# A two-block transformer kernel on one core: x in two transfers, setup moved into the first feed-forward, and another order at each feed-forward entry

## The chip, the core and the metric

The kernel runs on one core of a Trainium2 chip. A core has five engines with instruction streams of their own: TensorE (PE, matrix products and transposes), VectorE (DVE), ScalarE (ACT), GpSimd (POOL) and SyncE (SP), which here only issues transfers. Engines wait for each other by semaphores. Transfers come from HBM through 16 DMA engines, from one queue for those that SyncE issues and one for those of ScalarE. The metric is the device time of one execution in microseconds (us), less is better.

## What is computed

The input x has 256 tokens of 1024 values in fp32. Two layers of a first block and two layers of a second block follow each other. Each layer is a gated feed-forward (hidden width 2816), a mixer and another feed-forward, so there are eight feed-forwards.

```python
def first_block(x, ...):
    cos, sin = rope_tables(positions)
    for layer in range(DEPTH):
        x = x + 0.5 * swiglu(rmsnorm(x, norm_g[layer, 0]), ffn_w_gate[layer, 0], ffn_w_up[layer, 0], ffn_w_down[layer, 0])
        x = x + hybrid_mixer(rmsnorm(x, norm_g[layer, 1]), cos, sin, w_in[layer], ...)
        x = x + 0.5 * swiglu(rmsnorm(x, norm_g[layer, 2]), ffn_w_gate[layer, 1], ffn_w_up[layer, 1], ffn_w_down[layer, 1])
...
def second_block(x, ...):
    for i in range(DEPTH):
        f = swiglu_ffn(rmsnorm_2(x, ffn1_norm_pre[i]), ffn1_w_in[i], ffn1_w_out[i])
        x = x + 0.5 * rmsnorm_2(f, ffn1_norm_post[i])
        ...
        x = x + rmsnorm_2(y, mix_norm_post[i])
        f = swiglu_ffn(rmsnorm_2(x, ffn2_norm_pre[i]), ffn2_w_in[i], ffn2_w_out[i])
        x = x + 0.5 * rmsnorm_2(f, ffn2_norm_post[i])
```

The second block has a post norm: the output of a feed-forward or mixer is normed before it is added to x.

## The kernel before

**Split products.** Every fp32 operand is split into a high part (rounded to fp32r) and a low part (the rest), and each product is three: high by high, low by high, high by low (`three`, L505 to L507). Weights stream through a ring of four slots in parts of 128 x 1024 values (512 KB). For each part SyncE issues the transfers (`load_parts`, L344) once the slot's earlier low part is made; ScalarE makes the high part `wh` (`high`, L533) when the part has landed and TensorE has started on the part three before it (the semaphore `used`); VectorE, or GpSimd from the mixers to part 3 of the next feed-forward, makes the low part `wl` (`low`, L541). The helpers take a count: `high(e, t, 2)` makes the next two parts. The Python order of the calls is the order of the instructions on each engine; there is no scheduler.

**The entry of a feed-forward.** x lies with tokens on partitions, as two halves of 128 tokens (q = 0, 1). TensorE transposes 8 blocks of each half (`pe_xt`, L638). ScalarE makes their high parts `xh` (`act_xh`, L1279, four or eight of 128 x 128 at once) and VectorE their low parts `xl` (`dve_xl`, L1782). It starts on four low parts when the four high parts are there. Then chunk 0 (the first 256 of 2816 hidden columns, four weight parts, 0 to 3) runs for q = 0, then for q = 1; the transposes of the half q = 1 stand among the parts of q = 0, behind part 1 in the first block and behind part 2 in the second. Meanwhile ScalarE sums the squares of x (`act_sum`, L1283) and takes the root (`act_root`, L1289, L1292), and loads the table of silu (`tables`, L1257). TensorE goes on with part 4 (chunk 1) and then transposes the hidden values of chunk 0 (`turn`, L661), for which ScalarE has to apply silu (`silu`, L1361) and VectorE has to multiply by the up half (`gated`, L1861). Behind that ScalarE and VectorE make `hh` and `hl` of the hidden values (`turned`). Ten more chunks and 22 down parts follow.

**The residual in the second block.** In the entries behind a mixer or feed-forward with a post norm, ScalarE squares the output in PSUM (`act_post`, L1283), VectorE multiplies it by the post gains (`gained`, L1805) and adds it to x (`added`, L1813). TensorE's transposes of that half of x wait for the addition. This holds for three feed-forward entries, at 1852, 2048 and 2632 us.

**The setup.** SyncE loads x in one transfer of 1 MB and then weight parts 0 to 3. ScalarE issues eleven small transfers: positions and lambda parameters (spread to all partitions, 128 and 256 KB), norm gains (24 KB), and eight others. VectorE computes the rotary angles (L2026 to L2041) and lambda; TensorE transposes the gains (L1204) and the small parameters (L1206), both behind the wait for all parameters, and then the first half of x; ScalarE takes two sines (L1708, L1709), copies gains and parameters, takes two exponentials (L1716, L1717), and only then starts on weight parts.

## Time and profile before

| | us |
|---|---|
| median of three runs | 2831.6 |
| lowest and highest | 2831.0 and 2835.13 |
| the profiled execution | 2832.48 |
| its span | 2830.7 |

| engine | busy us | share of the span |
|---|---|---|
| TensorE products (PE) | 2733.8 | 97% |
| VectorE (DVE) | 1580.8 | 56% |
| ScalarE (ACT) | 1463.0 | 52% |
| GpSimd (POOL) | 899.4 | 32% |

The DMA engines move 450 MB, 159 GB/s on the mean. The chain of work that ended last is 87% TensorE. Times in rows are from the start of the span; the profiled execution took 1.8 us more than its span.

### The profile page before, as it was taken

How to read it: one execution, taken by the hardware profiler on the slowest of the kernel's cores; microseconds unless marked ns; L12 is line 12 of the kernel's file. 1: busy time of each engine (PE TensorE's matmuls, PEld its weight loads, DVE VectorE, ACT ScalarE, POOL GpSimd, SP SyncE). 2: the span in 40 equal slices, each digit the busy share in tenths (PEclk: the TensorE clock that was granted, in tenths of full speed). 3: DMA queues.
4: the chain of work that ended last, by engine and by line, in shares of the span. 5: the costliest groups of instructions: out<-in, count | busy, mean ns of one | idle time of the engine just before them, and what ended most of it. 6: DMA issues, size and time to landing. Idle time of an engine off the chain costs nothing.

```text
span 2830.7 us, 46605 instructions
## 1 busy us (share of the span) xinstructions
PE 2733.8 (97%) x17368; PEld 2360.3 (83%) x17368; DVE 1580.8 (56%) x2439; ACT 1463.0 (52%) x2136; POOL 899.4 (32%) x469
## 2 busy tenths in 40 slices
PE   7999999999999999999989999999999899999999
PEld 6888897887878997878879899878778798998787
DVE  5543854545544844545546585655455466756554
ACT  5445565445445655445455644654454556446543
POOL 0007563001017666010028554720100285547200
PEclk9999999999999999999999999999999999999999
DMA  5555445655555446556558542456555585424664
GB/s 183 184 182 153 132 138 178 186 186 176 185 167 156 132 142 193 186 172 191 184 137 201 113 91 73 148 183 186 176 182 185 139 197 120 91 69 149 186 186 142
DMA packets 368426, 450.01 MB, mean 159 GB/s; under 512 B 32510, under 2 KB 266112, under 8 KB 368224
## 3 DMA queue, kind: packets, MB, share of 16 engines
q1 hardware_dynamic: 366896, 446.34, 53.6%
q8 instruction: 138, 2.26, 0.3%
q10 hardware_dynamic: 400, 0.43, 0.1%
q0 software_dynamic: 928, 0.45, 0.1%
q14 instruction: 64, 0.52, 0.1%
HBM read 446.06 MB, written 1.05 MB: 158 GB/s over the span
## 4 chain that ended last, share of the span: by engine, by line
PE 87%; DVE 5%; ACT 4%; POOL 2%; issue 1%; DMA 0%; ACTq 0%; DVEq 0%
PE PS L505 26%; PE PS L507 25%; PE PS L506 25%; POOL wl L541 2%; PE PS L661 1%; ACT wh L533 1%; ACT xh L1279 1%; DVE PS L2078 1%; DVE wl L541 1%; PE PS L1072 1%; PE PS L770 1%; PE PS L1007 1%; PE PS L1139 1%; PE PS L638 1%; PE PS L998 1%
## 5 line engine op out<-in xcount | busy, mean ns | idle before, releaser
L541 POOL TENSOR_TENSOR wl<-ring,wh 128x1024 fp32r<-128x1024 f32 (+1 forms) x348 | 835.9, 2421 | 1728.5 <-ACT wh L533 1727.4
L533 ACT ACTIVATE wh<-ring 128x1024 fp32r<-128x1024 f32 x848 | 890.4, 1055 | 919.2 <-PE PS L505 880.4
L541 DVE TENSOR_TENSOR wl<-ring,wh 128x1024 fp32r<-128x1024 f32 x500 | 611.8, 1225 | 630.8 <-ACT wh L533 630.7
L505 PE MATMUL PS<-wh,xh 128*128 128x512 f32 x1600 | 634.0, 396 | 33.2 <-DVE xl L1782 25.3
L507 PE MATMUL PS<-wh,xl 128*128 128x512 f32 x1600 | 623.2, 390 | 0.0
L506 PE MATMUL PS<-wl,xh 128*128 128x512 f32 x1600 | 622.1, 389 | 0.0
L505 PE MATMUL PS<-xh,wh 128*128 128x256 f32 x1888 | 554.4, 294 | 1.7 <-DVE xl L1782 1.7
L506 PE MATMUL PS<-xl,wh 128*128 128x256 f32 x1888 | 539.3, 286 | 0.0
L507 PE MATMUL PS<-xh,wl 128*128 128x256 f32 x1888 | 538.9, 285 | 0.0
L505 PEld LDWEIGHTS PS<-wh,xh 128*128 128x128 f32 x1600 | 301.2, 188 | 101.5 <-issue 34.9
L505 PEld LDWEIGHTS PS<-xh,wh 128*128 128x128 f32 x1888 | 367.0, 194 | 22.5 <-issue 16.2
L506 PEld LDWEIGHTS PS<-xl,wh 128*128 128x128 f32 x1888 | 367.6, 195 | 2.5 <-issue 2.4
L507 PEld LDWEIGHTS PS<-xh,wl 128*128 128x128 f32 x1888 | 367.2, 195 | 0.0
L507 PEld LDWEIGHTS PS<-wh,xl 128*128 128x128 f32 x1600 | 301.1, 188 | 63.0
L506 PEld LDWEIGHTS PS<-wl,xh 128*128 128x128 f32 x1600 | 301.7, 189 | 58.1
L505 PE MATMUL PS<-wh,hh 128*128 128x512 f32 x704 | 279.1, 396 | 0.0
L507 PE MATMUL PS<-wh,hl 128*128 128x512 f32 x704 | 278.1, 395 | 0.0
L506 PE MATMUL PS<-wl,hh 128*128 128x512 f32 x704 | 278.1, 395 | 0.0
L2078 DVE SCALAR_TENSOR_TENSOR PS<-W,cols,PS 128x256 f32<-128x256 f32 x464 | 187.2, 480 | 0.0
L507 PEld LDWEIGHTS PS<-wh,hl 128*128 128x128 f32 x704 | 132.1, 188 | 32.1
L506 PEld LDWEIGHTS PS<-wl,hh 128*128 128x128 f32 x704 | 132.2, 188 | 31.7
L505 PEld LDWEIGHTS PS<-wh,hh 128*128 128x128 f32 x704 | 132.2, 188 | 31.5
(296 smaller groups left out, 2604.6 us busy)
## 6 DMA issues: line engine op xcount, KB each, us to landing
ring<-in_ffn_w_in_dram SPq DMA_DIRECT2D x352, 256.0 KB, 3.0
ring<-in_mix_w_in_dram SPq DMA_DIRECT2D x256, 256.0 KB, 3.8
ring<-in_w_in_dram SPq DMA_DIRECT2D x200, 256.0 KB, 3.0
ring<-in_ffn_w_gate_dram SPq DMA_DIRECT2D x176, 256.0 KB, 2.9
ring<-in_ffn_w_up_dram SPq DMA_DIRECT2D x176, 256.0 KB, 3.1
ring<-in_ffn_w_down_dram SPq DMA_DIRECT2D x176, 256.0 KB, 2.7
ring<-in_ffn_w_out_dram SPq DMA_DIRECT2D x176, 256.0 KB, 2.7
ring<-in_w_branch_dram SPq DMA_DIRECT2D x32, 256.0 KB, 2.9
```

Source lines behind the costliest of these rows:

```text
L505: first_ = mm(o, w[0], x[0], start=start, stop=False, skip_group_check=True)
L506: mm(o, w[0], x[1], start=False, stop=False, skip_group_check=True)
L507: return first_, mm(o, w[1], x[0], start=False, stop=stop, skip_group_check=True)
L533: act_(dst, src, ACT.Copy).then_inc(hi_ready, 1)
L541: (engine or v_).tensor_tensor(dst, src, part_views(t, wh)[0], ALU.subtract).then_inc(lo[t.slot()], 1)
L638: ins = nc.tensor.transpose(xt_bank(q, k), src[:, q, k * P:(k + 1) * P], ident[:])
L661: ins = nc.tensor.transpose(bank(4 + c % 2, o, o + P), act2[:, c % 2, q, j * P:(j + 1) * P], ident[:])
L770: mm(bank(5, 0, n), rot[:], ybuf[:, c % 2, 0:n], start=True, stop=True).then_inc(tr[0].sem, tr[0].did("rot." + name))
L998: ins = mm(PS[0:4, 4, 0:S], pick[:, 3 - h:7 - h], sq[:, 4 * (n % 2) + h, :], start=(h == 0), stop=(h == 3))
L1007: ins = mm(bank(4, i * S, (i + 1) * S), ident[0:4, h:h + 1].to_broadcast([4, P]), rstd[0:4, 0, 0:S], start=True, stop=True)
L1072: ins = mm(PS[r, 3 + 2 * c, h * HD:(h + 1) * HD], src[c][r, h, :], ident[r, r], start=True, stop=True)
L2078: ins = v_.scalar_tensor_tensor(conv[:, b, :] if tap == TAPS - 1 else part, src, w, part, ALU.mult, ALU.add)
```

## The change

1. x comes in two transfers of 512 KB: SyncE loads the half q = 0 first, ScalarE issues the load of q = 1 behind its first high weight part. Each half has its semaphore.
2. The norm gains are ScalarE's first transfer and have a semaphore of their own. Positions and lambda parameters are issued in the first entry, behind high part 3.
3. TensorE transposes the gains, then x (q = 0), then the small parameters, then runs chunk 0. ScalarE loads the table with exp and ln first, copies the gains and starts on weight parts; it copies the small parameters inside the entry.
4. The angles are computed by VectorE in chunks 3 to 5 of the first feed-forward, the lambda products in chunk 6; the sines follow on ScalarE in chunk 8, the exponentials and the rest of lambda in the down projection.
5. In the first entry weight and activation parts alternate: high part 0, xh of q = 0 in two groups of four with high part 1 between them, then high parts 2 and 3.
6. In the other seven entries ScalarE makes all eight xh of q = 0 in one go and high part 3 behind them. In all eight, one high part and one low part that stood ahead of chunk 0's silu and gating now stand behind them.
7. In the three entries with a post norm VectorE's multiplication by the post gains for q = 1 moves behind xl 4 to 7.

```diff
         def _(sp):
-            sp.dma_start(x, a["x"].rearrange("a (t p) d -> p (a t) d", p=P)).then_inc(x_in, 16)
+            load_x(sp, 0)
...
+            pe.wait_ge(gains_in, 16)
+            for k in range(KB):
+                ins = nc.tensor.transpose(bank(1, k * ROWS1, (k + 1) * ROWS1), rows[0:ROWS1, k * P:(k + 1) * P],
+                                          ident[0:ROWS1, 0:ROWS1])
+            ins.then_inc(pro_pe.sem, pro_pe.did("gains"))
+            pe_xt_ffn(pe, 0, 0)
             pe.wait_ge(params_in, N_PARAM)
-            for k in range(KB):
-                nc.tensor.transpose(bank(1, k * ROWS1, (k + 1) * ROWS1), rows[0:ROWS1, k * P:(k + 1) * P],
-                                    ident[0:ROWS1, 0:ROWS1])
...
             if s == 0:
                 high(e, t, 1)
-            if post:
-                post(0)
-            high(e, t, 2)
-            act_xh(e, s, 0, range(4), gain)
-            high(e, t, 1)
-            act_xh(e, s, 0, range(4, KB), gain)
+                load_x(e, 1)
+                act_xh(e, s, 0, range(4), gain)
+                high(e, t, 1)
+                act_xh(e, s, 0, range(4, KB), gain)
+                high(e, t, 2)
+                load_late(e)
+                e.wait_ge(params_in, N_PARAM)
+                e.wait_ge(pro_pe.sem, pro_pe.at("small"))
+                act_(small[:], bank(3, 0, SMALL), ACT.Copy).then_inc(pro_act.sem, pro_act.did("small"))
+            else:
+                if post:
+                    post(0)
+                high(e, t, 2)
+                act_xh(e, s, 0, range(KB), gain)
+                high(e, t, 1)
...
             high(e, t, 1)
-            if s == 0:
-                tables(LN_EXP)
             act_root(e, tr, env.lay, f"{tag}.ss1", tag, 0, QT)
             tables(SILU_TANH)
-            high(e, t, 2)
+            high(e, t, 1)
...
-                high(e, t, 2)
+                high(e, t, 3 if c == 1 else 2)
                 turned(c - 1)
+                chunk(c)
...
             if s == 0:
-                low(e, t, 3)
+                low(e, t, 1)
             gained(0)
             added(0)
             dve_xl(e, s, 0, range(4), gain)
             if s == 0:
                 low(e, t, 1)
-            gained(1)
             if s < 3 * LAYERS + 1:
+                gained(1)
                 added(1)
             dve_xl(e, s, 0, range(4, KB), gain)
+            if s == 0:
+                low(e, t, 1)
+                e.wait_ge(x_in[1], 16)
+                e.sem_inc(x_upd, 2)
+                low(e, t, 1)
             if s > 3 * LAYERS:
+                gained(1)
                 added(1)
             dve_xl(e, s, 1, range(KB), gain)
-            low(e, t, 3)
+            low(e, t, 2)
...
-                low(e, t, 2)
+                low(e, t, 3 if c == 1 else 2)
                 turned(c - 1)
+                chunk(c)
```

The order of instructions on ScalarE at the program's start, before. W, small and cols hold the setup's values, masks the sines and cosines, wh the high parts of the weights:

```order
L1708 ACT_TABLE_LOAD
L1708 ACTIVATE masks<-W 128x256 [waits setup_vector]
L1709 ACTIVATE masks<-W 128x256
L1712 ACTIVATE cols<-PS 128x48 [waits setup_products,params_loaded]
L1714 ACTIVATE small<-PS 128x14
L1716 ACT_TABLE_LOAD
L1716 ACTIVATE W<-W 128x4 [waits setup_vector]
L1717 ACTIVATE gd<-gd 8x2
L533 ACTIVATE wh<-ring 128x1024 [waits weight_parts_used,weights_landed_0,setup_scalar]
```

The same place after the change:

```order
L1268 ACT_TABLE_LOAD
L1728 ACTIVATE cols<-PS 128x48 [waits setup_products]
L543 ACTIVATE wh<-ring 128x1024 [waits weight_parts_used,weights_landed_0,setup_scalar]
L332 DMA x<-in_x_dram 128x1024
L1290 ACTIVATE xh<-PS,cols 128x128 [waits activations_transposed] x4
L543 ACTIVATE wh<-ring 128x1024 [waits weight_parts_used,weights_landed_1]
L1290 ACTIVATE xh<-PS,cols 128x128 [waits activations_transposed] x4
L543 ACTIVATE wh<-ring 128x1024 [waits weight_parts_used,weights_landed_2]
L543 ACTIVATE wh<-ring 128x1024 [waits weight_parts_used,weights_landed_3]
L308 DMA W<-in_positions_dram 128x256
L308 DMA W<-in_lambda_params_dram 128x512
L1354 ACTIVATE small<-PS 128x14 [waits setup_products,params_loaded]
```

Five operations and a table load stand no more between the first copies and the first weight part; three transfers now stand between parts and activations.

VectorE at the last entry, the one at 2632 us, before (post multiplication L1805, addition L1813, xl L1782, low weight parts L541, gating L1861):

```order
L1782 SCALAR_TENSOR_TENSOR xl<-PS,cols,xh 128x128 [waits activation_high_parts_made] x4
L1805 TENSOR_TENSOR PS<-PS,post 128x512 [waits second_norm_scalar]
L1805 TENSOR_TENSOR PS<-PS,post 128x512
L1782 SCALAR_TENSOR_TENSOR xl<-PS,cols,xh 128x128 [waits activation_high_parts_made] x4
L1813 SCALAR_TENSOR_TENSOR x<-PS,rs,x 128x512 [waits second_norm_vector,second_norm_scalar]
L1813 SCALAR_TENSOR_TENSOR x<-PS,rs,x 128x512 [waits second_norm_vector]
L1782 SCALAR_TENSOR_TENSOR xl<-PS,cols,xh 128x128 [waits activation_high_parts_made] x8
L541 TENSOR_TENSOR wl<-ring,wh 128x1024 [waits weight_high_part_ready] x3
L1861 SCALAR_TENSOR_TENSOR act<-PS,rs,act 128x256 [waits second_ffn_scalar] x2
L541 TENSOR_TENSOR wl<-ring,wh 128x1024 [waits weight_high_part_ready] x2
```

The same place after the change:

```order
L1807 SCALAR_TENSOR_TENSOR xl<-PS,cols,xh 128x128 [waits activation_high_parts_made] x8
L1830 TENSOR_TENSOR PS<-PS,post 128x512 [waits second_norm_scalar]
L1830 TENSOR_TENSOR PS<-PS,post 128x512
L1838 SCALAR_TENSOR_TENSOR x<-PS,rs,x 128x512 [waits second_norm_vector,second_norm_scalar]
L1838 SCALAR_TENSOR_TENSOR x<-PS,rs,x 128x512 [waits second_norm_vector]
L1807 SCALAR_TENSOR_TENSOR xl<-PS,cols,xh 128x128 [waits activation_high_parts_made] x8
L551 TENSOR_TENSOR wl<-ring,wh 128x1024 [waits weight_high_part_ready] x2
L1892 SCALAR_TENSOR_TENSOR act<-PS,rs,act 128x256 [waits second_ffn_scalar] x2
L551 TENSOR_TENSOR wl<-ring,wh 128x1024 [waits weight_high_part_ready] x3
```

The second group of four xl moved ahead of the post multiplication, and one low weight part moved behind the gating.

ScalarE at the same entry, before (high weight parts L533, xh L1279, square of the output L1283):

```order
L533 ACTIVATE wh<-ring 128x1024 [waits weight_parts_used,weights_landed_0]
L1279 ACTIVATE xh<-PS,cols 128x128 [waits activations_transposed] x4
L533 ACTIVATE wh<-ring 128x1024 [waits weight_parts_used,weights_landed_1]
L1279 ACTIVATE xh<-PS,cols 128x128 [waits activations_transposed] x4
L1283 ACTIVATE act,ss<-PS 128x1024 [waits second_mix_products]
```

And after:

```order
L543 ACTIVATE wh<-ring 128x1024 [waits weight_parts_used,weights_landed_0]
L1290 ACTIVATE xh<-PS,cols 128x128 [waits activations_transposed] x8
L543 ACTIVATE wh<-ring 128x1024 [waits weight_parts_used,weights_landed_1]
L1294 ACTIVATE act,ss<-PS 128x1024 [waits second_mix_products]
```

The second group of four xh moved ahead of a high weight part.

## Rows read from the trace of the kernel before

**Rows 1.** What TensorE waited for, whole span: us in total, times, longest us.
```profile
PE PS L505 <- DVE xl L1782: 27.0, 16, 5.3
PE PS L661 <- DVE act L1861: 9.2, 8, 2.1
```

**Rows 2.** Timeline of the start: start, duration, instruction, count, [idle before <- releaser].
```profile
2.21 0.74 SPq L344 DMA_DIRECT2D ring<-in_ffn_w_up_dram  x1
...
11.42 1.01 PE L1204 MATMUL PS<-ident,W 6*128 6x6 f32 x8 [8.90 <-DMA W<-in_diff_subln_g_dram]
...
12.96 1.28 ACT L1716 ACT_TABLE_LOAD   x1
...
14.58 2.95 ACT L533 ACTIVATE wh<-ring 128x1024 fp32r<-128x1024 f32 x3
...
19.74 0.77 PE L505 MATMUL PS<-wh,xh 128*128 128x512 f32 x1 [5.29 <-DVE xl L1782]
...
39.07 0.63 PE L661 MATMUL PS<-ident,act 128*128 128x128 f32 x4 [2.13 <-DVE act L1861]
```

**Rows 3.** Transfers issued in 0 to 3 us; last line 17 to 24: KB, us to landing.
```profile
x<-in_x_dram SPq DMA_DIRECT2D x1, 1024.0 KB, 7.7
ring<-in_ffn_w_up_dram SPq DMA_DIRECT2D x1, 256.0 KB, 9.0
W<-in_positions_dram ACTq DMA_DIRECT2D x1, 128.0 KB, 5.8
...
ring<-in_ffn_w_up_dram SPq DMA_DIRECT2D x4, 256.0 KB, 3.7
```

**Rows 4.** Stretches: length, busy time (instructions) of PE, PEld, DVE, ACT, POOL; clock, DMA, GB/s.
```profile
5.00:10.00 5.00, 0.00 (x0) 0.00 (x0) 3.07 (x10) 1.28 (x1) 0.40 (x2) 1.00 0.98 345
...
40.00:60.00 20.00, 20.00 (x91) 16.53 (x90) 11.37 (x14) 10.40 (x14) 0.00 (x0) 1.00 0.69 213
```

**Rows 5.** Timeline of the last entry with a post norm, 2630 to 2652 us.
```profile
2630.81 1.14 ACT L1279 ACTIVATE xh<-PS,cols 128x128 fp32r<-128x128 f32 x4 [0.45 <-PE PS L638]
...
2632.48 0.47 PE L505 MATMUL PS<-wh,xh 128*128 128x512 f32 x1 [1.28 <-DVE xl L1782]
...
2633.05 1.06 ACT L533 ACTIVATE wh<-ring 128x1024 fp32r<-128x1024 f32 x1 [1.09 <-PE PS L505]
...
2635.01 1.04 ACT L1283 ACTIVATE act<-PS 128x1024 f32<-128x1024 f32 x1
...
2636.18 1.30 DVE L1805 TENSOR_TENSOR PS<-PS,post 128x512 f32<-128x512 f32 x2 [3.06 <-ACT act L1283]
...
2637.87 0.47 PE L505 MATMUL PS<-wh,xh 128*128 128x512 f32 x1 [2.39 <-DVE xl L1782]
...
2638.41 1.40 DVE L1813 SCALAR_TENSOR_TENSOR x<-PS,rs,x 128x512 f32<-128x512 f32 x2
...
2640.28 0.48 PE L505 MATMUL PS<-wh,xh 128*128 128x512 f32 x1
...
2644.07 1.10 ACT L533 ACTIVATE wh<-ring 128x1024 fp32r<-128x1024 f32 x1
...
2650.27 0.87 DVE L1861 SCALAR_TENSOR_TENSOR act<-PS,rs,act 128x256 f32<-128x256 f32 x2
...
2651.29 0.63 PE L661 MATMUL PS<-ident,act 128*128 128x128 f32 x4 [1.20 <-DVE act L1861]
```

**Rows 6.** The same stretch of the entry at 1852 us: timeline, then the stretch's busy times.
```profile
1858.09 0.76 PE L505 MATMUL PS<-wh,xh 128*128 128x512 f32 x1 [2.38 <-DVE xl L1782]
...
1861.88 0.48 PE L505 MATMUL PS<-wh,xh 128*128 128x512 f32 x1
...
1858.00:1860.00 2.00, 1.91 (x5) 1.55 (x6) 2.00 (x5) 0.00 (x0) 0.00 (x0) 0.50 0.78 257
```

**Rows 7.** First hidden transposes at two entries of the other kinds, timeline.
```profile
471.23 0.63 PE L661 MATMUL PS<-ident,act 128*128 128x128 f32 x4 [0.71 <-DVE act L1861]
...
1287.54 0.63 PE L661 MATMUL PS<-ident,act 128*128 128x128 f32 x4 [1.29 <-DVE act L1861]
```

More of the change, by code:

```diff
@@ L238, in program @@
         passed = {e: sem(f"wait_passed_{e}") for e in ("sync", "vector", "tensor", "gpsimd", "scalar")}
-        x_in = sem("x_loaded")
-        pos_in = sem("positions_loaded")
+        x_in = [sem(f"x_loaded_{q}") for q in range(QT)]
+        gains_in = sem("gains_loaded")
+        late_in = sem("positions_and_lambda_loaded")
         params_in = sem("params_loaded")
@@ L312, in load_params @@
             ld = loader(q, params_in)
[L313 to L314 removed]
+            loader(q, gains_in)(rows[0:3 * LAYERS, :], a["norm_g"].rearrange("l r d -> (l r) d"))
             ld(gd[0:8, 0, 0:LAYERS], a["gdn_a_log_2"].rearrange("l h -> h l"))
             ld(gd[0:8, 1, 0:LAYERS], a["gdn_dt_bias_2"].rearrange("l h -> h l"))
[L317 removed]
             for l in range(LAYERS):
@@ L1329, in act_mix_in, with act_ffn @@
             act_xh(e, s, 1, range(KB), gain)
-        def act_ffn(e, t, ff, tr, s, tag, gain, post=None, midway=lambda: None, more=1):
+        def act_ffn(e, t, ff, tr, s, tag, gain, post=None, midway=lambda: None, more=1, chunk=lambda c: None):
             if s == 0:
                 high(e, t, 1)
-            if post:
-                post(0)
-            high(e, t, 2)
-            act_xh(e, s, 0, range(4), gain)
-            high(e, t, 1)
-            act_xh(e, s, 0, range(4, KB), gain)
+                load_x(e, 1)
[13 more added lines that the diff above has]
+                high(e, t, 1)
             if post:
@@ L1733, in _ @@
                 g1 = cols1[:, :, 3 * lay:3 * lay + 3]
-                act_ffn(e, t, first["ffn"], tr, s, "f0", lambda k: g1[:, k, 0:1])
+                act_ffn(e, t, first["ffn"], tr, s, "f0", lambda k: g1[:, k, 0:1], None, decays if lay == 0 else lambda: None,
+                        1, angles if lay == 0 else lambda c: None)
                 act_mix_in(e, t, tr, s + 1, lambda k: g1[:, k, 1:2])
@@ L1836, in dve_mix_in, with dve_ffn @@
             dve_xl(e, s, 1, range(KB), gain)
-        def dve_ffn(e, t, ff, tr, s, tag, gain, update=None, midway=lambda: None):
+        def dve_ffn(e, t, ff, tr, s, tag, gain, update=None, midway=lambda: None, chunk=lambda c: None):
             gained, added = update or (lambda q: None, lambda q: None)
             if s == 0:
-                low(e, t, 3)
+                low(e, t, 1)
             gained(0)
@@ L2248, in _ @@
             dve_setup(e)
-            e.wait_ge(pro_act.sem, pro_act.at("small"))
+            e.wait_ge(pro_act.sem, pro_act.at("cols1"))
             def halves():
@@ L2264, in _ @@
                 t = Tiles(lay * (T1 // SLOTS), 4 if lay else 0)
-                dve_ffn(e, t, ff, tr, s, "f0", lambda k: g1[:, k, 0:1], update)
+                dve_ffn(e, t, ff, tr, s, "f0", lambda k: g1[:, k, 0:1], update,
+                        (lambda: dve_lambda(e)) if lay == 0 else lambda: None,
+                        (lambda c: dve_angles(e, c)) if lay == 0 else lambda c: None)
                 dve_mix_in(e, tr, s + 1, lambda k: g1[:, k, 1:2], dve_residual(e, ff[0], "f0.dn", lay))
```

81 lines of the change are left out of this document (46 added, 35 removed).

## The prediction

> **What bounds the kernel now.** I read three views in this order. First the table of busy time above: TensorE is busy 97% of the span, so the end moves only where TensorE stands still or runs at its lower clock. Then the list of what TensorE waited for: its two largest entries that this change can touch are waits for low parts of the activations (L1782, 16 times, 27.0 us) and for the gated hidden values (L1861, 8 times, 9.2 us) [rows 1]. Then the timeline at each of the eight feed-forward entries. At the program's start the first transposes wait 8.9 us for the last parameter transfer (11.42), ScalarE loads a table at 12.96, splits its first weight part only at 14.58, and the first product runs at 19.74 [rows 2]. Behind the start, each entry has one wait ahead of the first hidden transposes (L661), and the three entries whose residual update goes through a post norm have a wait of 2.4 us in the middle of chunk 0 [rows 5, 7].
>
> **Part 1, the start.** Removed from the path: the rotary angles, the lambda steps, two sine activations and one table load no longer stand ahead of ScalarE's first high part, and TensorE's gain transposes wait for one 24 KB transfer, not for all eleven. What is late next is weight part 0. Its second half was issued at 2.21 and landed 9.0 us later [rows 2, 3], at 11.2. It stood behind 1 MB of x and 384 KB of positions and lambda rows (128 and 256 KB). Now half of x and those 384 KB come later, about 0.91 MB less, and the queues moved 345 GB/s in this stretch [rows 4]: 2.6 us, so 8.6. From there the path to the first product is one high part 1.06 (as at 2633.05 [rows 5]), the new issue of the second half of x on ScalarE's queue, about 0.5 (an issue took 0.74 on SyncE [rows 2]), and from the start of the four high activation parts to the first product 1.67 (2630.81 to 2632.48 [rows 5]): 3.2 us. First product near 11.9, against 19.74: **7.8 us**. Ends: if part 0 lands as late as now, 14.4 and 5.3 us; if it lands as the refills later do, 3.7 us after issue [rows 3], 9.1 and 10.6 us. I take the middle, because the queue is full either way.
>
> Three new waits stand in that path. The gains: the positions, 128 KB and first on the same queue, landed after 5.8 us, at 6.6 [rows 3]; 1.0 for eight transposes and 0.2 for the copy give 7.9, under 8.6. The remaining small parameters, for which TensorE now waits just before its first product: they landed by 11.4 with 384 KB ahead of them, so at most 11.4 now, under 11.9. The second half of x, issued near 10.2: 3.7 to 7.7 us to landing [rows 3] gives 13.9 to 17.9. VectorE waits for it, with low part 3 and the low activation parts of the second token half queued behind, and TensorE reaches the second transposes 12 products after the first. The first product lasts 0.77 as the one at 1858.09 does (0.76), where the granted clock is 0.50, the 1.2 GHz level, and five products fill 1.91 us [rows 2, 6]; 12 at about 0.4 us end at 16.7. So it costs nothing to 1.2 us; I take nothing, since half the bytes of the 7.7 us row are asked for.
>
> The Trainium skill speaks against this split: "DMA: Bandwidth & Descriptors", Bandwidth, asks for transfers of at least 1 MiB, and its fit (2.0 us plus bytes over 436 GB/s) makes two halves 2.0 us dearer in sum than one whole. No row here prices the halves. Were that fixed part on the path, the forecast would be 2809.8; as the second half lands under chunk 0, I leave it out.
>
> **Part 2, the setup that moves into chunks 3 to 8 of the first feed-forward.** Some 13 VectorE steps, two sine activations and, in the down projection, seven more small steps. In a steady stretch of 20 us VectorE is busy 11.4 and ScalarE 10.4 under 20.0 of TensorE [rows 4], so 8.6 us lie free in less than two chunks, against 1 to 1.5 us added in one. Cost nothing; without this cover they would cost their own length, some 5 us in all. The order shows no table load for the sines where they now stand. Nobody needs the angles before the mixer, and GpSimd, which waits for the cosine, starts its own low parts only there.
>
> **Part 3, one high part and one low part behind the gate, in all eight entries.** Before, ScalarE made parts 5 and 6 and VectorE low parts 4, 5, 6 before the first gating; now part 6 goes behind it. From the start of high part 4 (2644.07) to the end of the gating (2650.27 + 0.87) 7.07 us pass [rows 5]. Without one high part (1.06) it is 6.0. TensorE arrives at the transposes at 2651.29 - 1.20 = 2650.09, which is 6.02 us after 2644.07. With 0.15 from gating to transposes about 0.1 of the wait stays. The three first-block entries like the one at 471.23 (0.71) lose their wait whole [rows 7]: 3 x 0.7 = **2.1**. The entry at 1287.54 (1.29 [rows 7]) gives **1.1**; the three later ones, of which the last with 1.20 is shown [rows 5], give **1.1 each**. In the first feed-forward the wait of 2.13 [rows 2] goes, since one table load goes too: **2.1**. Low part 6 is then made some 1 us after the gate, while TensorE wants it two parts (over 5 us) later, so nothing is late next.
>
> The Trainium skill ("ScalarE: Activation LUTs", What ACT_TABLE_LOAD costs, and the terms) gives a table load about 2.7 us; the load here took 1.28 [rows 2], so the trace differs, and it decides. By 2.7 the 6.0 us chain would be 7.4 and each entry would keep 1.4 of wait, and this part would give nothing.
>
> **Part 4, high parts of the whole first token half in one go, and the post gains behind the low parts, in the three post-norm entries.** Before, low activation parts 4 to 7 stood behind the post gain on VectorE (2636.18, 1.30), which waited for ScalarE's square (2635.01), which waited for high weight part 3 and four high activation parts. That made the 2.39 wait at 2637.87 [rows 5]. Now ScalarE makes the four high parts straight after the first four, in the 1.09 us in which it stood idle before 2633.05; so weight part 3 is not later and the square is 1.0 earlier, at 2634.0. VectorE makes the low parts by 2634.2, in its own idle time (3.06 before 2636.18). The gain goes to 2635.2, the addition, which no longer waits for four low parts, to 2636.4 instead of 2638.41, and ends at 2637.8. TensorE runs without the wait to about 2636.7 and is then stopped by this addition at the second transposes. The product behind them starts 0.47 after the addition (2638.41 + 1.40 to 2640.28), so at 2638.2: **2.0 us** per entry, not 2.4, because the new wait takes the place of part of the old one. In the entry at 1858.09 the same stretch took 3.79 us (1858.09 to 1861.88) against 2.41 (2637.87 to 2640.28), at a granted clock of 0.50 [rows 5, 6]. With a pause under 1 us in place of 2.4 I expect the clock to stay up: **1.4** more.
>
> **Sum.** Start 7.8 + 2.1 = 9.9; first block 2.1; then 1.1; 1858: 2.0 + 1.4 + 1.1 = 4.5; the last two 3.1 each. Together 23.8. The profiled execution took 2832.48, so 2808.7 there; on the median of the three runs, 2831.6, it is **2807.8**.
>
> **Rivals.** *Late weights* (15%): part 0 lands as late as now, because its slices on the 16 engines wait for the slowest engine and not for bytes. For: 1.97 MB stood ahead up to its landing, at 345 GB/s less than the 11.2 us it took. Against: x itself landed by 8.5. Then 2.5 more, 2810.3. *Clock* (15%): shorter waits move everything behind them, and the falls of the clock move too. One fall costs 1.4 [rows 6]; three more make 2812.0, three fewer 2803.6. What speaks for it is that the entry at 1858 fell and its twins did not, though the wait was the same. The Trainium skill, "TensorE: Matmul & The Clock Gate", What's actually happening, says that the place of a change depends on a phase that a kernel doesn't set; the unequal twins agree. *Gate no earlier* (6%): the activation then waits for something else, a product or a landing, and Part 3 brings nothing, 8.6 less: 2816.4. Against it the products of the second token half end one part (2.7 us) before the transposes. *Slower* (2%): with an earlier start TensorE stays at 1.2 GHz in the first feed-forward. A chunk lasts about 11.4 us there and would cost some 9 more; from three chunks on the gain is eaten: 2835. Against it, after the first dozen products it never fell in the first block. *Not as said*: if the second half of x lands after 17.9, TensorE waits at the second transposes and the start brings up to 3 less, within the range.
>
> **How the numbers follow.** Forecast 62%, its own range 2805.0 to 2810.3 by the two ends of the start. The range goes to three fewer falls and to three more with late weights added in part: 2802.5 to 2814. About 0.2%, 5.7 us, is what a measurement of this kernel tells from no change. Faster by more than that 0.95, within 0.03, slower 0.02; all but the last rival are faster.
>
> **What would show it.** First product between 9.1 and 14.4; table load before the first high part gone; no wait over 0.3 us at L661's successors; in the three post-norm entries no wait in the middle of chunk 0 but a short one, 0.5 to 1, before the second transposes; granted clock 1.00 near 1850. Wrong would be a first product after 15, or entries that keep their waits.

## The result and the profile after

| | before | after |
|---|---|---|
| undisturbed executions, us | 2831.0 to 2835.13 | 2803.77, 2805.36, 2807.67 |
| the profiled execution | 2832.48 | 2807.67 |
| its span | 2830.7 | 2805.9 |

The ratio of after to before is 0.9905, with a 95% interval of 0.9885 to 0.9924, so 22 to 33 us are gone by the interval, 24.8 between the two profiled executions. One further execution of the changed kernel was disturbed and is left out. The forecast was 2807.8 with a range of 2802.5 to 2814: the median of the three, 2805.36, and the profiled execution lie inside it. The signs of the terms were right, but the sizes of several were not, and they cancelled in part. The rest of this text is about those.

The page of the changed kernel first: busy time of each engine with its share and instructions, and the chain that ended last.

```profile
PE 2735.0 (97%) x17368; PEld 2363.6 (84%) x17368; DVE 1588.1 (57%) x2439; ACT 1459.5 (52%) x2134; POOL 899.6 (32%) x469
...
PE 90%; DVE 4%; ACT 3%; POOL 2%; issue 1%; DMA 0%; SPq 0%; DVEq 0%; ACTq 0%
```

TensorE is about as busy as before (2735.0 us, before 2733.8), and the span is 24.8 shorter. So the time came out of its pauses, and the chain now runs over TensorE for 90% of the span, not 87%. Next, what TensorE waited for in the changed kernel (us in total, times, longest). The lines L505, L638, L661 and L1782 of before are L515, L648, L671 and L1807 now.

```profile
PE PS L648 <- DVE sq L1800: 18.1, 6, 3.8
PE PS L515 <- DVE xl L1807: 15.7, 12, 1.6
...
PE PS L1219 <- DMA W<-in_diff_subln_g_dram: 1.9, 1, 1.9
PE PS L648 <- DVE x L1838: 0.9, 3, 0.3
...
PE PS L1214 <- DMA W<-in_norm_g_dram: 0.5, 1, 0.5
```

Against [rows 1]: the waits for xl fell from 27.0 to 15.7 us, and the waits of the hidden transposes for the gated values, 9.2 us in eight entries, are gone from the list. Three waits of 0.3 for the residual addition (L1838) are new. Then the start, as a timeline (start, duration, instruction, count, idle before and what ended it), to be held against [rows 2].

```profile
3.01 1.02 PE L1214 MATMUL PS<-ident,W 6*128 6x6 f32 x8 [0.50 <-DMA W<-in_norm_g_dram]
...
7.21 1.06 ACT L543 ACTIVATE wh<-ring 128x1024 fp32r<-128x1024 f32 x1 [1.65 <-issue]
7.23 0.36 ACTq L332 DMA_DIRECT2D x<-in_x_dram  x1
8.18 1.12 ACT L1290 ACTIVATE xh<-PS,cols 128x128 fp32r<-128x128 f32 x4
...
8.38 1.23 DVE L551 TENSOR_TENSOR wl<-ring,wh 128x1024 fp32r<-128x1024 f32 x1 [5.67 <-ACT wh L543]
...
9.52 1.12 DVE L1807 SCALAR_TENSOR_TENSOR xl<-PS,cols,xh 128x128 fp32r<-128x128 f32 x4
...
10.01 0.77 PE L515 MATMUL PS<-wh,xh 128*128 128x512 f32 x1 [1.42 <-DVE xl L1807]
...
15.14 1.03 PE L648 MATMUL PS<-ident,x 128*128 128x128 f32 x8
```

The first product runs at 10.01, where it ran at 19.74. The second transposes at 15.14 have no wait, so the second half of x was there in time. The transfers issued early in the program (KB each, us from issue to landing):

```profile
x<-in_x_dram SPq DMA_DIRECT2D x1, 512.0 KB, 3.5
ring<-in_ffn_w_up_dram SPq DMA_DIRECT2D x1, 256.0 KB, 5.0
...
x<-in_x_dram ACTq DMA_DIRECT2D x1, 512.0 KB, 5.7
W<-in_lambda_params_dram ACTq DMA_DIRECT2D x1, 256.0 KB, 6.8
W<-in_positions_dram ACTq DMA_DIRECT2D x1, 128.0 KB, 4.8
```

The first two lines are of transfers issued in 0 to 3 us, the other three of later ones. The half of weight part 0 that landed last, issued at 2.16, took 5.0 us, where it took 9.0 from 2.21 on [rows 2, 3]. The second half of x was issued at 7.23 and was in at 12.9.

Last the entry with a post norm that stands at 2632 us in the kernel before:

```profile
2610.99 0.47 PE L515 MATMUL PS<-wh,xh 128*128 128x512 f32 x1 [1.27 <-DVE xl L1807]
...
2612.53 1.01 ACT L1294 ACTIVATE act<-PS 128x1024 f32<-128x1024 f32 x1
...
2613.65 1.30 DVE L1830 TENSOR_TENSOR PS<-PS,post 128x512 f32<-128x512 f32 x2 [1.00 <-ACT act L1294]
...
2614.86 1.40 DVE L1838 SCALAR_TENSOR_TENSOR x<-PS,rs,x 128x512 f32<-128x512 f32 x2
...
2615.66 1.32 PE L648 MATMUL PS<-ident,x 128*128 128x128 f32 x8 [0.30 <-DVE x L1838]
...
2616.73 0.47 PE L515 MATMUL PS<-wh,xh 128*128 128x512 f32 x1
```

The pause of 2.39 in the middle of chunk 0 [rows 5] is gone and one of 0.30 stands ahead of the second transposes. VectorE idles 1.00 ahead of the post gain, not 3.06.

Where the time was won, by the same instruction in both traces (before minus after, running sum): 9.7 at the first product, 12.15 at the first hidden transposes, 12.2 at 456 us, 14.0 at 1079, 14.9 at 1271, 16.5 at 1464, 16.4 at 1853, 21.25 at 2048, 24.5 at 2244, 24.3 at 2559, 21.5 at 2607, 21.5 at 2632, 24.8 at the end. Nearly all steps lie at entries, but for one loss of 2.8 just behind 2559.

### The profile page after: what moved, and what is told of

It reads as the page before. It is cut to its first block, busy times and chain, and to the rows that moved or that the text cites. A ratio compares the mean times of both kernels' runs of the same rounds, so it can differ in the third digit from the quotient of the medians.

```text
span 2805.9 us, 46606 instructions
## 1 busy us (share of the span) xinstructions
PE 2735.0 (97%) x17368; PEld 2363.6 (84%) x17368; DVE 1588.1 (57%) x2439; ACT 1459.5 (52%) x2134; POOL 899.6 (32%) x469
## 4 chain that ended last, share of the span: by engine, by line
PE 90%; DVE 4%; ACT 3%; POOL 2%; issue 1%; DMA 0%; SPq 0%; DVEq 0%; ACTq 0%
PE PS L515 27%; PE PS L517 26%; PE PS L516 26%; POOL wl L551 2%; PE PS L671 1%; DVE PS L2119 1%; ACT wh L543 1%; PE PS L1082 1%; PE PS L648 1%; PE PS L1149 1%; ACT xh L1290 1%; PE PS L780 1%; PE PS L1017 1%; PE PS L1008 1%; PE PS L1139 1%
## 5 line engine op out<-in xcount | busy, mean ns | idle before, releaser
L515 PE MATMUL PS<-wh,xh 128*128 128x512 f32 x1600 | 633.0, 396 | 22.3 <-DVE xl L1807 14.0
L515 PE MATMUL PS<-xh,wh 128*128 128x256 f32 x1888 | 554.9, 294 | 1.8 <-DVE xl L1807 1.7
L515 PEld LDWEIGHTS PS<-xh,wh 128*128 128x128 f32 x1888 | 367.4, 195 | 22.8 <-issue 16.1
L515 PEld LDWEIGHTS PS<-wh,xh 128*128 128x128 f32 x1600 | 301.0, 188 | 88.6 <-issue 20.6
L515 PE MATMUL PS<-wh,hh 128*128 128x512 f32 x704 | 279.3, 397 | 0.0
L515 PEld LDWEIGHTS PS<-wh,hh 128*128 128x128 f32 x704 | 132.3, 188 | 31.5
```

What stands on the lines that cost most here:

```text
L515: first_ = mm(o, w[0], x[0], start=start, stop=False, skip_group_check=True)
```

## Experiments

The edits below are against the kernel before or after, as said. Spans are those of the profiled execution, ratios are to the kernel before with the 95% interval. "Clock loss" is a sum of mine over 1 us stretches of one minus the granted clock, without the fall in which every trace ends: 25.6 us before, 27.3 after. It counts falls; it is not their exact price, for the one at 1858 cost 1.4 and counts 1.7.

**The changed kernel once more**, with nothing edited.

> The changed kernel once more, nothing edited. Theory: the waits of TensorE come out at the same places and sizes as in the first trace (first product at 10.0 us, no wait ahead of any first hidden transposes), while the falls of the granted clock in the second block lie elsewhere; the stretch from 2534 us to 2585 us, which was 2.8 us longer than in the kernel before because of a long fall at 2534 to 2541, is shorter again, so the span is 2803 us rather than 2805.9. Rival: the long fall belongs to the changed kernel (its new phase); then it is there again at the same place and the span is 2806 within 0.5.

Measured: median 2805.67, ratio 0.9911 (0.9894 to 0.9928), span 2803.0, clock loss 23.9. The span is 2.9 shorter than that of the same program above, and the clock loss 3.4 smaller. The stretch behind 2534 us shows half of this, first in the result's trace, then here (length, busy time and instructions of PE, PEld, DVE, ACT, POOL, granted clock, DMA share, GB/s):

```profile
2536.00:2538.00 2.00, 2.00 (x12) 2.00 (x11) 2.00 (x3) 1.16 (x2) 0.25 (x1) 0.50 0.31 78
2538.00:2540.00 2.00, 2.00 (x11) 2.00 (x11) 1.97 (x3) 1.04 (x2) 1.51 (x1) 0.50 0.54 193
2540.00:2542.00 2.00, 2.00 (x16) 2.00 (x15) 2.00 (x2) 1.40 (x2) 1.29 (x2) 0.79 0.00 0
```

```profile
2536.00:2538.00 2.00, 2.00 (x13) 2.00 (x13) 1.97 (x3) 1.46 (x3) 1.23 (x1) 0.62 0.64 228
2538.00:2540.00 2.00, 2.00 (x20) 2.00 (x19) 2.00 (x2) 2.00 (x4) 2.00 (x2) 1.00 0.01 2
```

The same instructions ran at 0.50, the 1.2 GHz level, until 2541 in one execution and until about 2537 in the other. Three of the kernels below that are the changed one but for its start (the covered setup, x whole, ScalarE on x first) have no fall there at all. So the 2.8 us that the changed kernel seemed to give back there are not a cost of the change: its executions differ by that much through the clock.

**The start alone** (after, with the entries 2 to 8 in their old order; their counts behind the first gating, not shown, go back too).

```diff
-                act_xh(e, s, 0, range(KB), gain)
-                high(e, t, 1)
+                act_xh(e, s, 0, range(4), gain)
+                high(e, t, 1)
+                act_xh(e, s, 0, range(4, KB), gain)
...
-            high(e, t, 1)
+            high(e, t, 1 if s == 0 else 2)
...
+            gained(1)
             if s < 3 * LAYERS + 1:
-                gained(1)
...
-            low(e, t, 2)
+            low(e, t, 2 if s == 0 else 3)
```

> The start alone: transfers, moved setup and the new order of the first feed-forward entry, the other seven entries as before. Theory (the parts add up): first product at 10.0, first hidden transposes at 26.9 without a wait, then everything as before, 12.2 us less than before, about 2819.8. Rival (the start also loses or gains later, by moved clock falls or refills of the ring): more than 2.5 us away from 2819.8.

Measured: 2821.66, ratio 0.9961 (0.9947 to 0.9975), span 2819.9, 10.8 shorter. The gain was 13.1 at 1401 us and 10.8 at the end: the clock loss was 29.0, 3.4 above before, with a longer fall near 1450 and a new one near 2628, behind a pause of 2.42. First product at 10.09, first hidden transposes at 26.05.

```profile
2626.16 0.47 PE L515 MATMUL PS<-wh,xh 128*128 128x512 f32 x1 [2.42 <-DVE xl L1808]
...
2628.00:2630.00 2.00, 2.00 (x10) 1.90 (x9) 0.23 (x2) 1.29 (x6) 0.00 (x0) 0.50 0.03 9
```

The start is worth its 12 to 13 us in its own stretch. The five executions took 2820.08 to 2821.86, all above the 2819.8 expected but within the 2.5 us of the rival. In the trace what is lost later stands at falls of the clock: 1.0 us between 1401 and 1850, 1.3 behind 2180. The entry at 2632 before [rows 5] had the same pause and no fall behind it.

**The other seven entries alone** (before, with the new order for s > 0; the lines are those of the two halves below).

> The seven later entries alone: start and first entry as before. Theory: the entries give 0.9 us three times, 1.6 once, 4.8 at 1852 us (1.4 of it from the clock) and 3.3 twice, 15.8 together, about 2816.2. Rival (the prediction's own terms, 0.7 three times, 1.1, 4.5, 3.1, 3.1): 13.9, 2818.1. If the clock is what matters, the sum differs by 2 to 3 us and the windows show it.

Measured: 2818.92, ratio 0.9957 (0.9940 to 0.9973), span 2815.5, 15.2 shorter, clock loss 23.9. In spans net of the clock loss the start gives 14.2, the entries 13.5, and the whole change 26.0 in the repeat that ran beside them. The sum is 1.7 too high. Most of this is in neither edit: TensorE reaches its fast clock level after fewer slow products in these two executions (the last section has the rows). The entries' kernel is 0.70 ahead at 25 us, before its first edited instruction, and at the first hidden transposes the start alone is 13.0 ahead where the repeat is 12.4. That makes 1.3, and 0.4 is left.

**The gate half of the entries** (before, one high and one low part behind the gating, for s > 0).

```diff
-            high(e, t, 2)
+            high(e, t, 1 if s else 2)
...
-                high(e, t, 2)
+                high(e, t, 3 if c == 1 and s else 2)
...
-            low(e, t, 3)
+            low(e, t, 2 if s else 3)
...
-                low(e, t, 2)
+                low(e, t, 3 if c == 1 and s else 2)
```

> The kernel before with one edit, in entries 2 to 8 only: one high part and one low part move from ahead of chunk 0's silu and gating to behind them (Part 3). Theory from the first trace of the change: each wait ahead of the first hidden transposes goes and takes with it about 0.17 us in which the products' tail empties, so 0.9 three times and about 1.4 four times, 8.3 together, 2823.5. Rival (the prediction's terms, 0.7 and 1.1): 6.5, 2825.3. The idle times in front of these transposes should be under 0.25 us.

Measured: 2827.52, ratio 0.9982 (0.9972 to 0.9991), span 2825.7, only 5.0 shorter. First what TensorE's hidden transposes waited for, then the two kinds of pause in its timeline:

```profile
PE PS L661 <- DVE act L1861: 2.3, 2, 2.1
...
1854.58 0.47 PE L505 MATMUL PS<-wh,xh 128*128 128x512 f32 x1 [2.40 <-DVE xl L1782]
...
2632.56 0.77 PE L505 MATMUL PS<-wh,xh 128*128 128x512 f32 x1 [2.41 <-DVE xl L1782]
```

Of the 9.2 us for the gated values [rows 1] 2.1 stay at the first entry, which this edit leaves alone, and 0.2 at one other. So the mechanism of Part 3 holds, in all seven entries. The time is worse than expected, by 4 us, and not in this execution alone: all ten lie above the 2823.5 expected, from 2825.67 on. In the trace the clock loss is 29.0, 3.4 above before, and net of it the span is 8.4 shorter. The pause of 2.4 in the entry at 1854 has no fall of the clock behind it now, and that at 2632 has one, the other way round than before [rows 5, 6]. That alone would change nothing; the 3.4 are two more falls, at 2049 behind the pause of the entry at 2046, and at 2554. Whether the edit brings such falls on in most executions one trace can't show.

**The order half** (before, all eight xh in one go and the post gain behind them, for s > 0).

```diff
             act_xh(e, s, 0, range(4), gain)
-            high(e, t, 1)
+            if s == 0:
+                high(e, t, 1)
             act_xh(e, s, 0, range(4, KB), gain)
+            if s:
+                high(e, t, 1)
...
-            gained(1)
             if s < 3 * LAYERS + 1:
+                gained(1)
                 added(1)
...
             if s > 3 * LAYERS:
+                gained(1)
                 added(1)
```

> The kernel before with the other edit of entries 2 to 8 only: eight xh in one go ahead of high part 3, and the post gain of q = 1 behind xl 4 to 7 (Part 4). Theory: 2.0 to 2.1 in each of the three post-norm entries, because the transposes of q = 1 wait for the addition, not for the low parts; 0.2 at 1274 us; nothing in the first block; with the fall of the clock at 1858 us gone, 1.4 more: 6.4 to 7.9, 2824 to 2825.5. The waits ahead of the first hidden transposes stay at 0.7 to 1.3. Rival: the whole 2.4 us of each wait is won, 8.6 or more.

Measured: 2825.51, ratio 0.9977 (0.9968 to 0.9987), span 2823.3; 7.4 shorter, with the clock loss as before (25.6).

```profile
1857.06 1.31 PE L638 MATMUL PS<-ident,x 128*128 128x128 f32 x8 [0.34 <-DVE x L1816]
...
1869.06 0.63 PE L661 MATMUL PS<-ident,act 128*128 128x128 f32 x4 [1.14 <-DVE act L1865]
...
2631.83 1.31 PE L638 MATMUL PS<-ident,x 128*128 128x128 f32 x8 [0.58 <-DVE x L1816]
```

The pauses of 2.4 are gone, a wait for the addition of 0.3 to 0.6 takes their place, and the waits for the gated values stay. So each half touches waits of its own, and the steps of the two add up entry by entry (the table under Parts 3 and 4 below).

**Only the xh order** (before, with the ScalarE lines of the last diff, VectorE as it was).

> The kernel before with only ScalarE's part of Part 4 in entries 2 to 8: eight xh in one go ahead of high part 3, VectorE's order as before, post gain of q = 1 ahead of xl 4 to 7. Theory: the square and with it gain, xl 4 to 7 and addition come 1.0 earlier, so the three waits in the middle of chunk 0 shrink from 2.4 to 1.4 and TensorE wins 1.0 in each, 3 to 4.5 with the clock, 2828. Rival (ScalarE's edit alone brings it all): the waits vanish and 2.0 each are won.

Measured: 2828.48, ratio 0.9986 (0.9976 to 0.9995), span 2825.3, as expected. The pauses of 2.4 are 1.38, 1.35 and 1.63:

```profile
1856.01 0.47 PE L505 MATMUL PS<-wh,xh 128*128 128x512 f32 x1 [1.38 <-DVE xl L1785]
...
2632.52 0.47 PE L505 MATMUL PS<-wh,xh 128*128 128x512 f32 x1 [1.63 <-DVE xl L1785]
```

About 1.0 of each pause (0.8 at the last) came from the high weight part ahead of the square on ScalarE, as Part 4 said. The rest, 1.4 to 1.6, came from the post gain ahead of the low activation parts on VectorE, less the new wait of 0.3 to 0.6.

**Is the moved setup covered?** (after, with fifteen more VectorE copies in chunks 4 to 8 of the first feed-forward.)

```diff
+            if 4 <= c <= 8:
+                for i in range(3):
+                    step(e, pr, v_.tensor_copy(posf, pos_i), f"extra{c}.{i}")
```

> The changed kernel with fifteen more VectorE operations of 128x256 (each about 0.3 us and waited for) in chunks 4 to 8 of the first feed-forward, three in each chunk, 5 us of VectorE time in all; the output is the same. Theory (moved setup is covered): no time, 2806.5 within 1.5, and no wait of TensorE above 0.15 us between 27 and 200 us. Rival (VectorE is near its limit there, the moved steps already cost something): up to 5 us more, 2811.

Measured: 2805.05, ratio 0.9911 (0.9895 to 0.9928), span 2802.3. The added work is there, three copies in each of five chunks,

```profile
64.01 0.94 DVE L2072 CAST W<-W 128x256 f32<-128x256 int32 x3
```

and between 27 and 200 us TensorE has no wait above 0.15. The lead over the kernel before is 12.9 us at the first hidden transposes and 13.0 at 153 us, so the added work cost nothing on the way. The cover that Part 2 names is real, with 4.7 us of more work under it.

**Four kernels on what sets the first product.** x whole: after, both halves of x issued by SyncE ahead of the weights. Late first: after, positions and lambda rows at the front of ScalarE's queue. Both: the two together.

```diff
             load_x(sp, 0)
+            load_x(sp, 1)
...
-                load_x(e, 1)
```

```diff
             ld = loader(q, params_in)
+            load_late(q)
...
-                load_late(e)
```

x whole:

> The changed kernel with both halves of x issued by SyncE ahead of the weights, as two transfers. Theory (bytes ahead of weight part 0 at 345 GB/s): part 0 lands 1.5 us later, the first product comes at 11.1 instead of 10.0 (0.4 of issue on ScalarE's queue is saved), about 2807.5. Rival (late weights: landing does not follow the bytes): first product at 10.0 or earlier.

Late first:

> The changed kernel with positions and lambda (384 KB) issued first on ScalarE's queue again. Theory: 1.1 us by bytes for weight part 0, and the gains, now behind them on the same queue, land at 6 to 8 us instead of 3.0; the first product comes at 11 to 12.5, about 2808. Rival: the queue of ScalarE takes turns with SyncE's and the small packets (1 to 2 KB) cost more than their bytes: first product at 13 or later.

Both:

> The changed kernel with all transfers at the start again (both halves of x ahead of the weights, positions and lambda first on ScalarE's queue), so that only the order of the compute is changed. Theory (bytes and queue positions): weight part 0 lands 3 to 4 us later than in the changed kernel, the first product comes at 13.0 to 14.4, about 3.5 us are lost, near 2809.5; so of the 9.7 us by which the first product moved some 6 belong to the moved compute and 3.5 to the transfers. Rival (the two transfer edits hide each other behind the later of the two paths): first product at 12.2, as with positions and lambda first alone.

| | first product | up half of part 0: issued, landed | gains transposed at | median | ratio |
|---|---|---|---|---|---|
| before | 19.74 | 2.21, 11.2 | 11.42 | 2831.6 | |
| after | 10.01 (repeat 9.41) | 2.16, 7.1 (repeat 6.5) | 3.01 (repeat 3.60) | 2805.67 (repeat) | 0.9911 |
| x whole | 11.54 | 2.63, 8.7 | 2.76 | 2806.91 | 0.9911 (0.9894 to 0.9927) |
| late first | 12.18 | 2.16, 9.1 | 8.08 | 2808.99 | 0.9915 (0.9898 to 0.9931) |
| both | 13.77 | 2.65, 10.9 | 8.24 | 2811.81 | 0.9926 (0.9909 to 0.9942) |

"Both" has the old bytes ahead of part 0 and the new order of computation, so it splits the 9.7 us: 6.0 come from the computation that left the path (19.74 to 13.77), 3.8 from the transfers (13.77 to 10.01), about the sum of 1.5 and 2.2 of the two singles. The transfers of one program vary too: with those of the changed kernel the half landed at 6.5 to 7.2 in five traces, so the 3.8 could as well be 4.4 (against the repeat). Its timeline shows the landing on the path. In "late first" it is another thing, the gains: the weights are there at 9.1, and ScalarE starts on them at 9.37, behind the copy of the gains that were transposed at 8.08.

```profile
8.24 1.02 PE L1216 MATMUL PS<-ident,W 6*128 6x6 f32 x8 [5.72 <-DMA W<-in_norm_g_dram]
...
10.97 1.06 ACT L545 ACTIVATE wh<-ring 128x1024 fp32r<-128x1024 f32 x1 [1.46 <-DMA ring<-in_ffn_w_up_dram]
```

```profile
8.08 1.02 PE L1215 MATMUL PS<-ident,W 6*128 6x6 f32 x8 [5.56 <-DMA W<-in_norm_g_dram]
```

With positions and lambda rows in front on the same queue, the gains, 24 KB, come 5.1 us later. The weight half lands 2.0 us later for these 384 KB, where the 512 KB of x cost it 1.5 (7.1 to 8.7; it is also issued 0.5 later there, behind the second half of x). Against the repeat these are 2.6 and 2.1. By bytes at 345 GB/s [rows 4] they would be 1.1 and 1.5. So x costs about its bytes, and the rows that are spread to all partitions cost nearly twice theirs. The stretches (as those above) show where that time goes, the first line before, the second after, the third "late first":

```profile
2.00:5.00 3.00, 0.52 (x2) 0.43 (x2) 0.00 (x0) 0.00 (x0) 2.05 (x11) 1.00 0.62 148
...
2.00:5.00 3.00, 2.12 (x13) 1.94 (x14) 0.16 (x1) 0.94 (x1) 2.05 (x11) 1.00 0.85 266
...
5.00:7.00 2.00, 0.00 (x0) 0.00 (x0) 0.00 (x0) 0.76 (x1) 0.40 (x2) 1.00 0.69 187
```

From 2 to 5 us the queues moved 148 GB/s before and 266 after, and in "late first" the DMA engines were busy for 0.69 of the time from 5 to 7 us, with weight parts still outstanding. A packet of the positions took 46 ns in the median there, as one of the weights of the same 1 KB did. So it isn't that their packets are slower; why engines stand idle beside them no run shows.

The end-to-end steps are small against the intervals, so here the rows carry the argument and the medians only agree in direction. The first product of "x whole" came 0.4 us later than expected, those of "late first" and "both" within their ranges; the median of "both" is 2.3 above the 2809.5 expected.

**ScalarE starts on x, not on the weights** (after, first entry: four xh, then high parts 0 and 1; VectorE likewise makes four xl and then low parts 0 and 1).

```diff
-                high(e, t, 1)
-                load_x(e, 1)
                 act_xh(e, s, 0, range(4), gain)
                 high(e, t, 1)
+                load_x(e, 1)
+                high(e, t, 1)
```

> The changed kernel with another order at the start: ScalarE makes xh 0 to 3 in the 1.65 us in which it waits for weight part 0, then high parts 0 and 1, then xh 4 to 7; VectorE makes xl 0 to 3, then low parts 0 and 1, then xl 4 to 7. Theory: the first product follows low part 0 alone, 7.2 + 1.1 + 1.2 = 9.5 instead of 10.0, half a us less, which the times cannot tell from nothing. Rival (something else stands ahead of the first product, the small parameters' transfer or transposes): still 10.0.

Measured: 2804.89, ratio 0.9901 (0.9884 to 0.9917), span 2801.8, first product at 9.28, first hidden transposes at 25.33. It uses the 1.65 us in which ScalarE idled ahead of its first high part, for it could make xh while part 0 was landing. From that landing to the first product 2.4 us pass, in both executions of the changed kernel 2.9, so 0.4 to 0.5 are won. It is the lowest of all medians, but its interval overlaps that of the changed kernel.

## Why the prediction was right, and where its sizes were off

**What bounds the kernel.** Right: TensorE's busy time stayed, only its pauses shrank.

**Part 1, the start: 12.15 measured, 9.9 forecast.** The mis-sized term is the landing of part 0. The sum charged 0.91 MB at 345 GB/s, 2.6 us, and took 8.6; it landed at 7.16, 4.0 us earlier than before. The first product, 10.01, is inside the ends of 9.1 and 14.4. The step that failed is "the middle, because the queue is full either way": 345 GB/s is the rate from 5 to 10 us, and from 2 to 5 us the DMA engines were busy for 0.62 of the time before and 0.85 after. Of the 4.0, x accounts for its bytes, 1.5, and positions and lambda rows for 2.0, not 1.1. Taken away together the two give 3.75 (10.89 in "both" to 7.14). The other 0.3, from 11.18 before to 10.89 with the same bytes ahead, is about the scatter of the five traces with the old transfers, 10.97 to 11.18. From landing to first product the sum had 3.2 us and the trace has 2.85: the issue on ScalarE's queue, charged with 0.5, cost nothing, as it stands at 7.23 beside the high part that runs from 7.21; against that VectorE was still at the first low weight part and came to xl at 9.52, 0.2 behind the end of xh (8.18 + 1.12). The gains, the small parameters (a wait of 1.92 that ended at 8.31) and the second half of x cost nothing, as said.

The Trainium skill, "DMA: Bandwidth & Descriptors", Bandwidth, spoke for transfers of at least 1 MiB, and the same page's fit, which it gives for transfers that GpSimd issues, puts 2.0 us on each transfer. Here the first half of x took 3.5 us where the whole had taken 7.7 [rows 3], and the second half landed under products. What the split costs in sum "both" shows, which has the old transfers but for it: the second half was in at 9.4, where the whole was in at 8.6 before, 0.9 later and not 2.0, and the weight half was no later.

From the first product to the first hidden transposes 19.33 us passed before and 16.91 after, 2.42 less, for a wait of 2.13 [rows 2]. The rest is the pipeline's tail, below, and the clock: the same stretch took 17.25 in the repeat and 15.96 with the start alone, so one trace gives the start's gain to about 1 us.

**Part 2, the moved setup: nothing.** Right, and with room for 4.7 us of VectorE's work at least.

**Parts 3 and 4 by entry.** The gain between the same instructions (before minus the kernel named, us) in two stretches of each entry. In the last two lines falls of the clock lie inside the gate half's stretch.

| entry, us in before | first to second transposes of x: after, order half, forecast | on to the first hidden transposes: after, gate half, forecast |
|---|---|---|
| 452 | 0.0, 0.0, 0 | 0.86, 0.86, 0.7 |
| 643 | 0.0, 0.0, 0 | 0.85, 0.86, 0.7 |
| 1075 | 0.0, 0.0, 0 | 0.86, 0.85, 0.7 |
| 1267 | 0.45, 0.46, 0 | 1.14, 1.12, 1.1 |
| 1850 | 3.42, 3.42, 3.4 | 1.38, 1.42, 1.1 |
| 2046 | 2.18, 2.18, 2.0 | 1.09, 0.18, 1.1 |
| 2630 | 2.19, 1.92, 2.0 | 1.08, 0.91, 1.1 |

**Part 3, behind the gate.** Right on which waits go. It was low in the first block, 0.86 where it had 0.7, for the sum took the idle time as the price. In the trace of before the last product ahead of [rows 7]'s first line starts at 470.14:

```profile
470.14 0.39 PE L507 MATMUL PS<-wh,xl 128*128 128x512 f32 x1
```

The transposes follow at 471.23, 1.09 later, and idle is counted only behind the product's 0.39. With no wait they start 0.24 after it, as here in the changed kernel:

```profile
26.68 0.40 PE L517 MATMUL PS<-wh,xl 128*128 128x512 f32 x1
...
26.92 0.60 PE L671 MATMUL PS<-ident,act 128*128 128x128 f32 x4
```

So the wait was worth 0.85, 0.71 and some 0.15 more. In the second block the 1.1 was right but for the entry at 1850. There the waits of 1.16 to 1.29 don't vanish whole, which is the 0.1 that the sum left over:

```profile
1270.54 0.39 PE L517 MATMUL PS<-wh,xl 128*128 128x512 f32 x1
1271.06 0.63 PE L671 MATMUL PS<-ident,act 128*128 128x128 f32 x4
```

The transposes start 0.52 behind the last product here and 0.38 behind it in the three later entries, not 0.24.

The Trainium skill ("ScalarE: Activation LUTs", What ACT_TABLE_LOAD costs) makes its 2.7 us up of two parts, the load of near 1.28 and a drain of near 1.38. The prediction took the 1.28 of the trace to be against the page. It is the page's figure for the load [rows 2]; what the trace lacks is the drain, for the activation behind that load starts at 14.25, 0.01 after its end. So the rival by which this part would have brought nothing is refuted: the load takes 1.28 in the changed kernel too, and the waits are gone.

**Part 4, the post-norm entries.** Right in mechanism: no pause in the middle, a new one ahead of the second transposes, 0.3 where 0.5 to 1 was expected. The first of the three gave its 3.4, the fall of the clock in it, the other two 2.2 where the sum had 2.0. Overlooked was the entry at 1267, which has no post norm: TensorE waited 0.20 for xl at 1274.12 there, and the eight xh in one go took that wait away too, worth 0.45. Part 3 and Part 4 together gave 4.8 at 1858 (forecast 4.5), 3.26 and 3.3 at the last two (3.1 each). The granted clock is 1.00 there, as forecast:

```profile
1834.00:1842.00 8.00, 6.40 (x35) 4.89 (x34) 4.76 (x12) 5.34 (x16) 6.06 (x3) 1.00 0.48 141
```

**The sum.** The steps add to 27.8, the forecast's to 23.8, and 24.8 came in the profiled execution. The difference of 3 is what the rival *Clock* described: falls at other places and of another length, above all the 2.8 behind 2534 us. So the closeness of 24.8 to 23.8 is luck: a start that was 2.2 too small and entries that were 1.8 too small in sum met a clock term of 3 that I had put at zero. The medians, 2805.36 and 2805.67 in the repeat, lie 2.4 and 2.1 under the forecast, which is nearer to what the terms were short of. That rival was true beside the forecast, not in place of it; a term of plus or minus 3 belongs in the range, as it stood, and its middle was not zero in this execution. The repeat, with 23.9 of clock loss, shows the other side: 27.7 us of gain in the span.

*Late weights* is refuted by the landing at 7.16, *Gate no earlier* by the row of the gate half, *Slower* by first-feed-forward products that keep 0.23 us distance from the fifteenth microsecond on, *Not as said* by the landing at 12.9.

## What to carry to other kernels

Price a wait that goes whole by the distance between the starts of the instructions around it, less their normal distance, not by the idle time in front of the second. At a program's start bytes over one rate is a poor price for a transfer ahead of the weights: 512 KB of x cost its bytes here, 384 KB of spread rows nearly twice theirs. Put what nobody needs yet behind the first weights, and compare landings, not times from issue, when an edit moves the issue too. Where pauses decide whether the clock falls, give the clock a term of its own in the range and settle its sign only with repeated traces of both kernels.

## What was not expected of the hardware

The clock losses of the thirteen traces differ by multiples of 1.7 us: they are 23.9, 25.6, 27.3 or 29.0, and the same program gave 27.3 and 23.9. The same wait of 2.40 us had a fall behind it at 1858 and none at 2638 before, and the other way round with the gate half alone. The Trainium skill, "TensorE: Matmul & The Clock Gate", What's actually happening, has the phase of a change outside a kernel's hand; these pairs agree.

At the program's start the granted clock reads 1.00 while products follow each other by 0.43 us, which is the distance at 0.50 [rows 6], five in 2 us. First the changed kernel, then the start alone, where the distance falls to 0.32 and then to 0.23:

```profile
10.00:12.00 2.00, 1.99 (x5) 1.61 (x6) 2.00 (x6) 2.00 (x6) 0.00 (x0) 1.00 1.04 359
```

```profile
12.36 0.63 PE L517 MATMUL PS<-wh,xl 128*128 128x512 f32 x1
12.79 0.49 PE L515 MATMUL PS<-wh,xh 128*128 128x512 f32 x1
13.11 0.39 PE L516 MATMUL PS<-wl,xh 128*128 128x512 f32 x1
```

This 1.00 is no measurement. The traces' record of the granted clock has its first entry at 14.98 us in the changed kernel, at 25.02 before and at 12.98 with the start alone, and the view writes 1.00 for what lies ahead of it. In all thirteen traces products ahead of the first entry follow each other by 0.43 or more and those behind it by 0.23, but for one or two at the change. So by their distance the first products run at the 1.2 GHz level, and the record begins with the rise.

Before that rise 12 products started in the kernel before and in both executions of the changed one, 9 in that of the entries, 7 with the start alone. Five products at 0.2 us each are the 1.0 us by which the first feed-forward of the start alone was shorter than that of the changed kernel, with the same instructions in it. A difference of 1 us at a program's start is therefore not to be put down to an edit on one trace.

What is left at the entries is a wait of 1.3 to 1.6 ahead of each first product, since VectorE starts on low parts only when four high parts are there. A finer handoff was not run: VectorE and ScalarE would then use the same PSUM bank with no order between them.
